# A two-layer decoder with seven-product gate/up pairs: three plain pairs and not four, and the first-half gate products of two later pairs made early

## The reference

```python
h = rms_norm(x, norm_gains[l, 2])
gu = h @ w_gate_up[l]
y = (jax.nn.silu(gu[..., :D_FF]) * gu[..., D_FF:]) @ w_down[l]
x = x + rms_norm(y, norm_gains[l, 3])
```

## Time and profile before

| | |
|---|---|
| Time, median of 3 runs | 2039.13 us (2037.52 to 2039.89) |
| Profiled execution: its time, its span | 2038.86 us, 2037.2 us |
| TensorE busy | 1989.5 us, 98% of the span, 9470 matmuls |
| VectorE, ScalarE, GpSimd busy | 1429.8, 894.0, 315.4 us |
| Mean granted TensorE clock | 0.996 |

### The profile page before, as it was taken

How to read it: one execution, slowest core, us unless ns; L and a number is a source line. 1 busy time by engine, 2 the same in 40 slices (tenths; PEclk the granted TensorE clock), 3 DMA queues, 4 the chain that set the end, 5 groups by cost and what they waited for, 6 DMA issues and landing times.

```text
span 2037.2 us, 25039 instructions
## 1 busy us (share of the span) xinstructions
PE 1989.5 (98%) x9470; PEld 1597.3 (78%) x9470; DVE 1429.8 (70%) x1861; ACT 894.0 (44%) x1481; POOL 315.4 (15%) x177
## 2 busy tenths in 40 slices
PE   8999999999999999999999999999999999999997
PEld 6776878888888878888777776688788888888886
DVE  6567686576788875666445467677789988875665
ACT  6446353445545354343444456836522222234341
POOL 3645000111211000000000001210224323300001
PEclk9999999999999999999999999999999999999999
DMA  5228841456688877666222222152256644476644
GB/s 178 101 73 301 301 140 47 160 207 217 231 295 306 299 263 242 209 236 229 83 83 83 83 67 59 43 179 85 96 196 230 226 177 165 174 294 248 221 153 162
DMA packets 122199, 363.64 MB, mean 178 GB/s; under 512 B 11616, under 2 KB 13024, under 8 KB 116832
## 3 DMA queue, kind: packets, MB, share of 16 engines
q1 hardware_dynamic: 105616, 331.89, 46.2%
q10 hardware_dynamic: 16464, 30.15, 4.3%
HBM read 241.28 MB, written 114.43 MB: 175 GB/s over the span
## 4 chain that ended last, share of the span: by engine, by line
PE 46%; DVE 4%; issue 2%; ACT 2%; DMA 2%; POOL 0%; SPq 0%; POOLq 0%; ACTq 0%; DVEq 0%
PE PS L1013 5%; PE PS L1014 5%; PE PS L1015 5%; PE PS L750 5%; PE PS L755 5%; PE PS L751 5%; PE PS L1031 3%; PE PS L1032 3%; PE PS L1033 3%; PE PSC L886 2%; PE PTR L916 2%; PE PX L903 2%; DMA inner<-TP 1%; DVE SS L1884 0%; DVE CL L2138 0%
## 5 line engine op out<-in xcount | busy, mean ns | idle before, releaser
L1031 PE MATMUL PS<-RP,DH 128*128 128x512 f32 x616 | 240.6, 391 | 3.0 <-DVE RP L2320 3.0
L1033 PE MATMUL PS<-RP,DL 128*128 128x512 f32 x616 | 239.8, 389 | 0.0
L1032 PE MATMUL PS<-RP,DH 128*128 128x512 f32 x616 | 239.7, 389 | 0.0
L1013 PE MATMUL PS<-BHT,SH 128*128 128x512 f32 x576 | 224.1, 389 | 0.0
L1014 PE MATMUL PS<-BLT,SH 128*128 128x512 f32 x576 | 224.1, 389 | 0.0
L1015 PE MATMUL PS<-BHT,SL 128*128 128x512 f32 x576 | 224.1, 389 | 0.0
L2771 POOL TENSOR_TENSOR WL<-WR,WH 128x1024 fp32r<-128x1024 f32 (+2 forms) x40 | 84.1, 2117 | 677.0 <-ACT WH L1178 669.5
L1013 PE MATMUL PS<-BH,SH 128*128 128x512 f32 x432 | 168.3, 389 | 1.6 <-DVE TP L2168 0.9
L1015 PE MATMUL PS<-BH,SL 128*128 128x512 f32 x432 | 168.1, 389 | 0.0
L1014 PE MATMUL PS<-BL,SH 128*128 128x512 f32 x432 | 168.1, 389 | 0.0
L1031 PEld LDWEIGHTS PS<-RP,DH 128*128 128x128 f32 x616 | 115.6, 188 | 28.0 <-DVE RP L2320 4.1
(11 more groups left out here) (349 smaller groups left out, 4602.5 us busy)
## 6 DMA issues: line engine op xcount, KB each, us to landing
SR<-in_wst SPq DMA_DIRECT2D x36, 1024.0 KB, 4.8
ZS<-in_wdn SPq DMA_DIRECT2D x32, 704.0 KB, 6.1
s_keep<-ZS SPq DMA_DIRECT2D x32, 704.0 KB, 4.7
DR<-s_keep SPq DMA_DIRECT2D x32, 704.0 KB, 5.3
inner<-TP SPq DMA_DIRECT2D x36, 512.0 KB, 4.4
WR<-in_w SPq DMA_DIRECT2D x35, 512.0 KB, 6.1
DR<-in_wdn SPq DMA_DIRECT2D x24, 704.0 KB, 5.3
RR<-t_keep SPq DMA_DIRECT2D x16, 1024.0 KB, 5.2
```

What stands on the lines that cost most here:

```text
L1013: MM(BANK[bank], SH[b][:, w, c], BH[t][:, k, :], start=(k == 0), stop=False)
L1031: MM(bank, wh[:, i, :], rh, start=(i == 0), stop=False)
L1032: MM(bank, wh[:, i, :], rl, start=False, stop=False)
L1033: ins = MM(bank, wl[:, i, :], rh, start=False, stop=(i == KD - 1))
```

## The change

Three plain pairs are left in each layer, and pairs 3 to 21, 19 of them, are done in seven products. For the first two of these (f = 3 and 4) products 0 and 2 are left out of `pair`. They are made beside the first token half as two new jobs ("early", between pairs 0 and 1), each with the gate's weights of that pair: the first four feature tiles into one bank, the other four into a second. ScalarE copies the first bank out (`early_copy`), VectorE adds the second to it (`early_add`), and SyncE keeps both tiles in DRAM (`keep_early`) and brings them back when the pair is done (`early_first_back`, `early_gate_back`). These two pairs split only one raw block and not three. The order of the lists around this follows, the slot rule of the pairs counts from the first pair, and the keeps of layer 1's down weight sums begin a pair later. The diff, cut:

```diff
-NHT = 4
+NHT = 3
 NPAIR = NF - NHT
+NEARLY = 2
...
-        jobs += [Job("ffn", l, (f, j), halves=(h,), tag=h, slot=2 * f + j if l else wide(2 * f + j),
-                     share=("ffn", l, (f, j), 0) if h else None)
-                 for h in range(2) for f in range(NHT) for j in range(2)]
-        jobs += [Job("st", l, f, slot=(f + l) % 2) for f in range(NHT, NF)]
+        run = [Job("ffn", l, (0, j), halves=(0,), tag=0) for j in range(2)]
+        run += [Job("early", l, f, halves=(0,)) for f in range(NHT, NHT + NEARLY)]
+        run += [Job("ffn", l, (f, j), halves=(0,), tag=0) for f in range(1, NHT) for j in range(2)]
+        for n, o in enumerate(run):
+            o.slot = n if l else wide(n)
+        slot_of = {o.i: o.slot for o in run}
+        jobs += run
+        jobs += [Job("ffn", l, (f, j), halves=(1,), tag=1, slot=slot_of[f, j], share=("ffn", l, (f, j), 0))
+                 for f in range(NHT) for j in range(2)]
+        jobs += [Job("st", l, f, slot=(f - NHT + l) % 2) for f in range(NHT, NF)]
...
+    if o.name == "early":
+        if o.l:
+            return ((5, 6), (0, 1))[o.i - NHT]
+        return 2 * (n % 2), 2 * (n % 2) + 1
     if o.name == "ffn" and o.l == 1:
-        return ((2 * o.i[0] + o.i[1]) % 4,)
+        return ((2 * (o.i[0] + o.tag) + o.i[1]) % 4,)
...
-            return (q + q // NPAIR) % 2
+            return (q % NPAIR + q // NPAIR) % 2
...
-                j, b, q = J[("st", l, f, None)], (f + l) % 2, NPAIR * l + f - NHT
+                j, q = J[("st", l, f, None)], NPAIR * l + f - NHT
+                b, early = pair_slot(q), is_early(q)
                 pe.wait_ge(st_lo, 2 * (q + 1))
                 if f == NHT:
-                    pe.wait_ge(t_lo, 4 * (l + 1))
+                    pe.wait_ge(t_lo, 4 * l + 3)
                 products = ((A11, "11"), (S2, "T2"), (A12, "21"), (S3, "T3"), (S1, "T1"), (A22, "T4"), (S4, "22"))
                 for n, (w, t) in enumerate(products):
                     bank = product_bank(q, n)
-                    if n < 4:
+                    if early and n in (0, 2):
+                        continue
+                    if n < 4 or early and n in (4, 6):
                         if bank in PS_WAIT[j]:
                             s, v = PS_WAIT[j][bank]
                             pe.wait_ge(named[s], v)
                     else:
                         pe.wait_ge(named[PRODUCT_READ[n - 4]], q + 1)
+                    if (f, n) == (NHT, 5):
...
-                        ins.then_inc(st_mm, 1)
+                        ins.then_inc(st_mm, 2 if early and n in (1, 3) else 1)
                     else:
                         ins.then_inc(mm_done, 1)
+
+            def early_job(l, f, hook=None):
+
+                j = J[("early", l, f, None)]
+                wh, wl = hi(j), lo(j)
+                begin(j)
+                for k in range(KT):
+                    bank, c = BANK[banks(j)[k // 4]], k % 4
+                    MM(bank, wh[:, k, :], bh(0, k), start=(c == 0), stop=False)
+                    MM(bank, wh[:, k, :], bl(0, k), start=False, stop=False)
+                    ins = MM(bank, wl[:, k, :], bh(0, k), start=False, stop=(c == 3))
+                    if k == KT - 1:
+                        ins.then_inc(mm_done, 1)
+                    if hook is not None:
+                        hook(2 * k + 1)
...
-                    places = {(0, 1, 0): {0: [("col", s_x, 0)], 4: [("row", s_x, 0)]},
-                              (0, 2, 0): {5: [("col", s_y, 1)]}, (0, 2, 1): {2: [("row", s_y, 1)]},
+                    early_places = {NHT: {0: [("col", s_x, 0)], 4: [("row", s_x, 0)]}}
+                    places = {(0, 1, 0): {5: [("col", s_y, 1)]}, (0, 1, 1): {2: [("row", s_y, 1)]},
                               (1, 1, 0): {5: [("col", s_x, 1)]}, (1, 1, 1): {0: [("row", s_x, 1)]}}
...
+                        if (h, f) == (0, 0):
+                            for e in range(NHT, NHT + NEARLY):
+                                early_job(l, e, after_k(early_places[e]) if e in early_places else None)
...
+            def early_copy(l, i):
+
+                j = J[("early", l, NHT + i, None)]
+                act.wait_ge(mm_done, j + 1)
+                A(EARLY_TILES[:, i, 0, :], BANK[banks(j)[0]], ACT.Copy).then_inc(p1_done, 1)
...
+                if q == 3:
+                    act.wait_ge(early_kept, early_kept_all(l))
...
+                a = A22 if is_early(q) else A11
                 act.wait_ge(*st_seen(q))
-                A(SH[pair_slot(q)][:, A11:S3, :], SR[pair_slot(q)][:, A11:S3, :], ACT.Copy).then_inc(st_hi, 1)
+                if q % NPAIR == 1:
+                    act.wait_ge(mm_done, J[("ffn", q // NPAIR, (NHT - 1, 1), 1)] + 1)
+                A(SH[pair_slot(q)][:, a:S3, :], SR[pair_slot(q)][:, a:S3, :], ACT.Copy).then_inc(st_hi, 1)
...
-                    gate(l, 1, 0)
-                    for k in range(4, KT):
-                        residual(r, 1, k)
+                    early_copy(l, 0)
+                    residual(r, 1, 4)
+                    residual(r, 1, 5)
+                    early_copy(l, 1)
+                    residual(r, 1, 6)
+                    residual(r, 1, 7)
...
+                    gate(l, 1, 0)
...
-                    gate(l, 3, 0)
+                    gate(l, 2, 0)
...
-                    gate(l, 1, 0)
+                    early_copy(l, 0)
                     weight_hi(ffn[6])
                     norm_root(s_y, 1)
+                    early_copy(l, 1)
                     weight_hi(ffn[7])
...
                         if k == 3:
-                            gate(l, 2, 0)
-                    gate(l, 3, 0)
+                            gate(l, 1, 0)
+                    gate(l, 2, 0)
...
-                    st_raw_hi(q0)
+                st_raw_hi(q0)
+                st_sum_hi(q0)
                 gate(l, 2, 1)
-                if l == 0:
-                    st_raw_hi(q0)
-                st_sum_hi(q0)
-                gate(l, 3, 1)
...
-                    p1_copy(q)
+                    if not is_early(q):
+                        p1_copy(q)
...
+            def early_add(l, i):
+
+                q = NPAIR * l + i
+                dve.wait_ge(p1_done, q + 1)
+                V.tensor_tensor(EARLY_TILES[:, i, 1, :], EARLY_TILES[:, i, 0, :],
+                                BANK[banks(J[("early", l, NHT + i, None)])[1]], ALU.add).then_inc(c11_done, 1)
...
+                    early_add(l, 0)
                     residuals(r, 1, (5, 6))
                     weight_lo(ffn[7])
-                    product(l, 1, 0)
+                    early_add(l, 1)
                     residuals(r, 1, (7,))
                     invert(s_x, 1)
                     normed(r, 1, range(4))
+                    product(l, 1, 0)
+                    normed(r, 1, range(4, KT))
                     product(l, 2, 0)
-                    normed(r, 1, range(4, KT))
-                    product(l, 3, 0)
...
-                    gate_scaled(1, 0)
-                    product(l, 1, 0)
+                    early_add(l, 0)
                     weight_lo(ffn[6])
                     invert(s_y, 1)
+                    early_add(l, 1)
                     weight_lo(ffn[7])
 
...
-                t_low(l, 3)
+                if l == 0:
+                    t_low(l, 3)
+                    st_add(q0)
                 product(l, 1, 1)
-                if l:
-                    gate_scaled(2, 1)
-                else:
-                    st_add(q0)
                 st_raw_lo(q0)
-                product(l, 2, 1)
                 st_sum_lo(q0)
                 if l:
-                    gate_scaled(3, 1)
-                product(l, 3, 1)
+                    t_low(l, 3)
+                    gate_scaled(2, 1)
+                product(l, 2, 1)
...
-                    c11(q)
+                    if not is_early(q):
+                        c11(q)
...
+                if q == NPAIR + 1:
+                    pool.wait_ge(mm_done, J[("ffn", 1, (NHT - 1, 0), 1)] + 1)
...
-                if PREV[j] is not None:
-                    sp.wait_ge(mm_done, PREV[j] + 1)
+                sp.wait_ge(mm_done, (J[("ffn", l, (1, 1), 1)] if f == NHT + 1 else PREV[j]) + 1)
                 sp.dma_start(SR[pair_slot(q)][:, 0:4, :], w_st[q].rearrange("p (b n) -> p b n", b=4)) \
-                    .then_inc(st_loaded[f % 2], 16)
+                    .then_inc(st_loaded[q % 2], 16)
+
+            def keep_early(l, i):
+
+                sp.wait_ge(c11_done, NPAIR * l + i + 1)
+                sp.dma_start(early_keep[:, i, :, :], EARLY_TILES[:, i, :, :]).then_inc(early_kept, 16)
+
+            def early_first_back(l, i):
+
+                if i:
+                    sp.wait_ge(u2_done, NPAIR * l + i)
+                else:
+                    sp.wait_ge(early_kept, early_kept_all(l))
+                    sp.wait_ge(mm_done, J[("ffn", l, (1, 1), 1)] + 1)
+                sp.dma_start(SCR[0][:, :], early_keep[:, i, 0, :]).then_inc(early_first, 16)
+
```

(50 more changed lines are left out.)

46 lines of the change are left out of this document (30 added, 16 removed).

## The result

The changed kernel took 2099.39 us (2098.56 to 2103.76, four runs) against 2038.91 us of the kernel before: a ratio of 1.0307, 95% interval 1.0294 to 1.0319. It is slower, as forecast, by 60 us and not by 46. The ratio on the time shown ahead gives 2101.7 us, 1.7 above the end of the range. Timed again later it took 2099.76 us, 1.0316 (1.0296 to 1.0336).

A forecast was written before the change was run, and what follows sets the result against it. TensorE, busy for 98% of the span, was taken as the bound: its instructions plus its gaps. Terms -5.4 - 3.0 - 2.0 + 37.7 + 6.4 + 2.6 + 3.9 + 0.8 + 5.1 = +46.1 on 2038.86 gave 2085 us, range 2068 to 2100.

The forecast's parts named there:

- The matmul count: Both layers' early pairs: 12 matmuls fewer per layer, 24 in all, -5.4 us.
- The hand-over: Last pair to down products: weights await its buffer; gaps 21.6 us (layer 0, C12) and 16.1 (layer 1, C21), +37.7.
- The start of the pairs in layer 1: First pair waits 7.3 us on VectorE's list against 0.87, +6.4; pair 2 waits on its load and sums, +2.6.
- Smaller terms: Layer 0's second-half statistics and layer 1's second early job, together +3.9 us; also -2.0 and +0.8 for other waits.
- the second early job: Layer 1: waits 3.2 us for bank 1, which VectorE must first read; +2.7 after absorbing a 0.5 wait.
- layer 0's early pairs: Splits of pairs 1 and 2 end 0.2 and 0.6 us late, +0.8 (0 to 4).
- layer 0's column sums: Second-half statistics: a later VectorE addition and one more operation in the chain, +1.2 us (0 to 2).
- the waits that should go: Later right-hand-block waits in the down stage, -3.0; a product held by a keep and one ahead of pair 1, -2.0.
- The clock: Half-clock restarts after three gaps longer than one of 2.35 us, each costing 1.7 us of TensorE's time: +5.1 (0 to 8).
- (a): Rival: down weights come in time, their buffer being free when the last pair starts; 2047 us, chance 0.04.
- (b): Rival: short hand-over, TensorE starts on the first blocks (12.7) and the rest flows, no clock term; 2068 us, chance 0.05.
- (c): Rival: crowded hand-over, landings grow to 8 us and the sum of waits reaches 55; 2102 us, chance 0.05.

The follow-up runs named there:

- The flip alone: Kernel before, with only its first two down weights of each layer put into the buffers that its last pair holds, end of layer 0 unchanged: 2077.29 us, 1.0190.
- the last three runs: Changed kernel with repaired buffers and banks, plus layer 1 feed-forward banks (2046.20 us), then VectorE's low parts reordered (2043.14), then second pair's load issued earlier (2045.50).
- the last run: The best version with one more edit: in layer 1 the second pair's load is issued before SyncE waits for the first plain pair's second half; 2045.50 us, 1.0032.
- the best version: Changed kernel with three repairs of a few lines, other layer 1 feed-forward banks, and layer 1 low parts made in the first pair's reading order: 2043.14 us, 1.0027.
- three repairs of a few lines: Changed kernel with free buffers for first down weights, layer 0's product banks rotated by three, layer 1's attention jobs in their former banks: 2052.75 us, 1.0072.

## Why the prediction was right in its main term, and where it failed

- *The matmul count*, -5.4: right, 9446 for 9470.
- *The hand-over*, +37.7: right in its cause, its stations and the two releasers, and measured at 24.0 + 17.3 = 41.3. The flip alone cost the kernel before 38 us. Landings were the mis-sized part: the blocks were split 1.6 to 2.5 us later than the trace of before suggested, inside the bounds given.
- *The start of the pairs in layer 1*, +6.4 and +2.6: 7.8 less 0.9 is +6.9, and pair 2 waited 2.0. The cause, VectorE's list, was shown by the last three runs. That 7.8 came so near 7.3 is luck. From the first difference tile to the end of the operation that frees the bank the list took 31.6 us, where the sum had 27.3 (TensorE, its earlier wait left out, came 20 us after the list's start, as in the sum), and part of the excess had been waited off before: the list already held up the last plain pair's job, 3.9 us where 1.5 stood, +2.4. The mis-sized term is GpSimd's share. The sum gave it 2.1 us and it took 6.4 (31.6 for 25.2), since its sums for the first pair stretched the differences too and those for the second pair ran into the rest. VectorE and GpSimd together:

```profile
1465.08 6.32 DVE L2271 TENSOR_TENSOR TFT<-YOA 128x2048 f32<-128x2048 f32 x2
1466.03 3.23 POOL L2917 TENSOR_TENSOR SR<-SR 128x512 f32<-128x512 f32 x1
...
1489.50 3.34 DVE L2302 TENSOR_TENSOR SL<-SR,SH 128x2048 fp32r<-128x2048 f32 x1
1490.77 3.19 POOL L2918 TENSOR_TENSOR SR<-SR 128x512 f32<-128x512 f32 x1
...
1496.03 0.68 DVE L2239 TENSOR_TENSOR TP<-PS,RSTD 128x512 f32<-128x512 f32 x1
```

- *Smaller terms*: the second early job 3.0 (3.2 forecast), layer 0's early pairs 1.6 (0.8), layer 0's column sums 0.9 more than before (1.2); of the waits that should go (-5.0) 3.8 went.
- *The clock*, +5.1: the step that failed first. Its count was wrong: I counted the three longest gaps, and rows behind seven waits show the half clock. Its price, 1.7 us, was right for five of them; behind two it was 3.0 and 3.1. What the clock cost is 11.9 us more than before. The row that the term rested on is itself a gap of 2.35 us, and the sum held waits of 3.2 and 2.6 us to which the term was not applied.
- *The attention stage*: the step that was not there. The sum went through the stages that the diff touches, and the only things it followed beyond them were two buffers. The same count that flipped the buffers (19 for 18) has a twin in the number of jobs ahead of layer 1 (95 for 96), and banks go by the parity of that number. That is a wait of 6.0 us; the wait of 2.3 us on softmax that stood there before is gone, so it adds 3.7 net.

Together the two misses are 6.8 and 3.7 us of the 18.7 by which span and sum differ (+64.8 and +46.1); the hand-over's 3.6, the 2.4 of the second half, the 1.2 of old waits that stayed and the 0.8 of the early pairs are the rest to within 0.2. In all, the steps that failed are the count of the clock's gaps and the stage that was not looked at.

The rivals: (a) is out, SyncE issued after the end; (b) is out, since C12 and C21 held the bank, though the kernel before with the flip showed in layer 1 what it looks like with a free bank (14.2); (c) asked for 55 us of waits and there were 41. (The high ends of the terms add up to 2109 and not 2108; nothing hangs on it.) My own row, 1.7 us behind a gap of 2.35, applied to those two waits of the sum as well, would have given 3.4 us more. The Trainium skill's rule on the clock (TensorE: Matmul & The Clock Gate, "Part 1: The HAM clock gate"), that TensorE is back at half clock after an idle stretch that is long enough, agrees with the rows behind the waits of 6.0 to 24.0 us. It does not settle the shorter ones, and there the rows decide: half clock behind 2.0, 3.0 and 3.9 us here and behind 2.35 in the kernel before, full clock behind its 2.16. The Trainium skill's rule on the shared port (SBUF — State Buffer, "Who interferes with whom") agrees with the last run, 2.28 us against 3.35 and 3.38.

Where the gain went, from the profiled execution of the best version (PE busy 1987.6, span 2038.9): matmuls -5.4; old waits on blocks and plain products -3.9; waits on VectorE in the pairs 8.5 where 1.6 stood, +6.9; column sums +1.0; low clock 1987.6 - 1984.1 = +3.5. Together +2.1, and its span is 1.7 us longer. Eleven us less of TensorE's work in the second half of layer 1 left VectorE's 25 us of differences, low parts and products uncovered, stretched by GpSimd's sums; no run took those sums out of the stretch, so what that would bring is open. The median of the best version is 5.5 us above that of the kernel before, because the two profiled executions are not typical: that of the best version is its fastest of seven, 2.4 us under its median, and that of the kernel before lies 1.2 us over the median measured beside this version.

## What to carry to other kernels

When an edit changes how many jobs or pairs there are, list everything that goes by a number's parity or remainder, buffers, banks and semaphore turns, through the whole program and not only in the stage that is edited; here that was three quarters of the loss (46.6 of 60.5 us came back with three repairs of a few lines). Moving matmuls away from a stage helps only while the engine that prepares the next one has slack there: count that engine's list before the stage is made shorter. Price the clock on every new wait from 2 us on: here most of them paid 1.4 to 1.9 us, two paid 3, and a few of about 2 us paid nothing.

## What the runs showed that I had not expected

- A load order may need more distance than the data: weights that came into buffers free three products ahead instead of four cost 4.5 + 7.1 us of waits and the low clock behind them, some 20 us in all by the medians, since ScalarE and VectorE stop at that weight in their lists.
- A wait removed ahead of a stage with a backlog is worth a part of itself: 7.2 us and the low clock behind it brought 2 to 4.5 us, too little to be told from noise by the times, and 1.6 at the first pair by the traces.
- VectorE's list was stretched by GpSimd's sums of two pairs, 6.4 us where the forecast had 2.1: a list gets longer when a neighbour's work for the next stage falls beside it.
- A wait on a bank was put down to GpSimd (6.0 us) in one profile and to "issue" (7.2 us) in another of the same kernel. In both it was VectorE's read of the bank; only the ends of the operations tell.
